# Eight-core decoder trunk: first input and weights without gates, first head in halves, last tile split

## What is computed

```python
def trunk(x, ...):
    for l in range(2):
        h = rmsnorm(x, norm_mix[l])
        if l == 0:   # pool channels (256) and six HGRN heads (128 x 128 state each)
            mixed, p_new, s_new = even_layer(h, ...)   # h @ w_in (1024 x 3328), pooling, recurrence, @ w_out
        else:
            mixed, c_new = odd_layer(h, ...)           # (B * conv3(C * hv)) @ w_out, with h @ w_in (1024 x 3072)
        x = x + mixed
        h = rmsnorm(x, norm_mlp[l])
        x = x + jnp.square(jax.nn.relu(h @ ff_w1[l])) @ ff_w2[l]      # 1024 -> 4096 -> 1024
    return rmsnorm(x, norm_final), ...
```

## Time and profile before

| what | value |
|---|---|
| median of 3 runs | 1538.13 us (1537.94 to 1538.3) |
| the profiled execution | 1537.33 us |
| its span, slowest core (core 4) | 1535.8 us |
| spans of the cores | 1529.1 to 1535.8 us |
| TensorE (PE) busy | 1455.6 us, 95%, 9034 matmuls |
| VectorE (DVE) busy | 887.7 us, 58% |
| ScalarE (ACT) busy | 632.0 us, 41%, 71 table loads of 1.283 us among it |
| GpSimd (POOL) busy | 186.0 us, 12% |
| chain that ended last | PE 90%, ACT 4%, DVE 3%, DMA 1% |

### The profile page before, as it was taken

The page is one execution under the profiler, slowest core; times in us unless marked ns, Lnnn a source line. Parts: engine busy times, 40 slices in busy tenths (PEclk is TensorE's granted clock), DMA queues, the critical chain, the costliest instruction groups (busy, mean ns, idle before and its releaser), DMA issues.

```text
span 1535.8 us, 24078 instructions; the slowest of 8 cores (1529.1 to 1535.8 us)
## 1 busy us (share of the span) xinstructions
PE 1455.6 (95%) x9034; PEld 817.6 (53%) x9034; DVE 887.7 (58%) x1860; ACT 632.0 (41%) x1187; POOL 186.0 (12%) x272
## 2 busy tenths in 40 slices
PE   2789799999999999999999999999999999999996
PEld 1445344554555444444444446666666666666663
DVE  4766686676657768565333368533357767433355
ACT  3788747655797433222212234222133224211132
POOL 1233313001111141100100010001001110001000
PEclk9899799999999999999999999999999999999998
DMA  6835333157346646962633558055245544155222
GB/s 142 183 56 83 56 56 85 28 114 166 83 85 140 152 70 99 174 117 52 110 56 61 104 111 167 15 97 85 51 72 83 95 89 83 25 86 95 52 58 75
DMA packets 49553, 138.56 MB, mean 90 GB/s; under 512 B 7840, under 2 KB 15904, under 8 KB 47904
## 3 DMA queue, kind: packets, MB, share of 16 engines
q0 software_dynamic: 29408, 101.76, 39.9%
q1 hardware_dynamic: 19600, 34.93, 6.9%
q10 hardware_dynamic: 432, 0.33, 0.1%
HBM read 223.21 MB, written 15.54 MB: 155 GB/s over the span
## 4 chain that ended last, share of the span: by engine, by line
PE 90%; ACT 4%; DVE 3%; DMA 1%; issue 1%; POOL 0%; DVEq 0%; SPq 0%; ACTq 0%; POOLq 0%
PE pp L549 89%; ACT arena L494 3%; DVE hT L529 1%; ACT L494 1%; DVE arena L514 1%; DMA x_sb<-xp 1%; DMA ring<-wst 1%; DVE arena L529 0%; POOL arena L514 0%; PE pp L558 0%; DVE arena L542 0%; DVE x_sb L514 0%; ACT mixT L494 0%; DVE mixT L514 0%; DVE mixT L529 0%
## 5 line engine op out<-in xcount | busy, mean ns | idle before, releaser
L549 PE MATMUL pp<-hT,ring 128*128 128x512 bf16 (+3 forms) x4320 | 785.5, 339 | 5.4 <-DVE hT L529 4.5
L549 PEld LDWEIGHTS pp<-hT,ring 128*128 128x128 bf16 x4320 | 408.5, 98 | 346.6 <-issue 24.9
L549 PE MATMUL pp<-mixT,ring 128*128 128x512 bf16 (+2 forms) x3200 | 576.0, 339 | 7.5 <-DVE mixT L514 4.5
L549 PEld LDWEIGHTS pp<-mixT,ring 128*128 128x128 bf16 x3200 | 311.4, 98 | 249.8 <-issue 17.1
L494 ACT ACTIVATE mixT<-pp 128x512 bf16<-128x512 f32 (+2 forms) x320 | 164.6, 514 | 485.2 <-PE pp L549 484.3
L514 DVE TENSOR_TENSOR x_sb<-x_sb,pp 128x512 f32<-128x512 f32 (+3 forms) x384 | 220.7, 579 | 199.0 <-PE pp L549 198.6
L514 DVE TENSOR_TENSOR mixT<-mixT 128x512 bf16<-128x512 bf16 (+2 forms) x320 | 119.3, 376 | 234.8 <-ACT mixT L494 233.9
L564 POOL DMA_DIRECT2D ring<-wst x202 | 107.7, 542 | 971.0 <-PE pp L549 957.2
L494 ACT ACTIVATE arena<-pp 128x512 f32<-128x512 f32 (+9 forms) x261 | 129.2, 508 | 160.2 <-PE pp L549 142.7
L494 ACT ACTIVATE arena<-x_sb 128x512 f32<-128x512 f32 (+3 forms) x184 | 97.6, 538 | 156.7 <-DVE x_sb L514 144.3
L514 DVE TENSOR_TENSOR arena<-arena 128x512 f32<-128x512 f32 (+6 forms) x195 | 114.3, 586 | 23.6 <-ACT arena L494 19.6
(11 more groups left out here) (65 smaller groups left out, 426.1 us busy)
## 6 DMA issues: line engine op xcount, KB each, us to landing
ring<-wst POOLq DMA_DIRECT2D x186, 512.0 KB, 9.0
arena<-st_hgrn SPq DMA_DIRECT2D x6, 1024.0 KB, 5.3
nhs<-arena SPq DMA_DIRECT2D x6, 1024.0 KB, 7.4
x_sb<-xp SPq DMA_DIRECT2D x8, 512.0 KB, 10.7
mixT<-xp SPq DMA_DIRECT2D x8, 512.0 KB, 7.8
ring<-wst POOLq DMA_DIRECT2D x16, 256.0 KB, 7.9
yp<-arena SPq DMA_DIRECT2D x16, 256.0 KB, 10.2
yp<-arena SPq DMA_DIRECT2D x16, 176.0 KB, 1.9
```

Source lines behind the costliest of these rows:

```text
L549: ins = e.matmul(o, l, r, start=s, stop=t)
```

## The change

It has four parts.

- **First input and first weights.** The first 512 tokens get a tensor of their own, xp0, in which what one load fetches is contiguous for each partition. The head weights are laid out by projection, f, i, g, q, 1024 columns each; head 0's come in four loads with a semaphore each. All gates at the start go; the staging of half 1's input (gate_x1) instead waits for head 5's weights, and the small wblk loads go behind head 0's.
- **First norm and first head.** The norm of each half of tile 0 (g_normx) sums its squares in parts by several matmuls; three of its eight products are made on GpSimd. Head 0's projections of tile 0 are made per half. Tile 1's norm adds on GpSimd.
- **Last tile.** In the last step (1728, 2064) becomes (1728, 1952) and (1952, 2064) with TCUT = 1952; both use g_norm_tail, which stores two chunks at a time, the last tile's on SP and ACT in turn, and ys in one store.
- **Planner.** New priorities, DMA rates of 300e3, and HB1 of 4 in place of 6.

The rest are details that keep buffers apart (a few added waits) and the new column offsets. The diff, cut:

```diff
-    PRI = {'norma': 0, 'frontA': 4.6, 'add': 8.7, 'pools': 10.8, 'normy': 59.0, 'cchain': 18.7, 'normc': 0, 'normz': 4.2, 'poolA': 3.1}
+    PRI = {'norma': 15.2, 'frontA': 4.6, 'add': 0, 'pools': 10.8, 'normy': 50.3, 'cchain': 18.7, 'normc': 0, 'normz': 1.3, 'poolA': 3.1, 'relu': 0, 'dense': 21.4, 'normp': 0, 'normd': 4.6, 'poolB': 0, 'normx': 4.5}
-    DMA_RATE = {"sp": 200e3, "act": 200e3, "pool": 270e3}
+    DMA_RATE = {"sp": 300e3, "act": 200e3, "pool": 300e3}
...
+    xp0 = din("xp0", [128, 2, 8, 256])
...
-        ring_ds = [new_dsem(f"ds_ring{i}") for i in range(NSLOT)]
+        ring_ds = [[new_dsem(f"ds_ring{i}_{q}") for q in range(4)] for i in range(NSLOT)]
...
-        HB1 = 6
+        HB1 = 4
...
+                st = 1024 if key == ("H", 0, 0) else 2048
+                for c0 in range(0, unit_cols[u], st):
+                    c1 = min(c0 + st, unit_cols[u])
                     pairs.append((ring[:, s, c0:c1], wst[u, :, c0:c1]))
-                yield DMA("pool", ring_ds[s], pairs, after_, [B_ring[s]], nbytes=unit_cols[u] * 512)
+                if key[0] == "H":
+                    for i, pr in enumerate(pairs):
+                        k = st // 1024
+                        if key == ("H", 0, 5):
+                            gate_x1.extend(B_ring[s])
+                        yield DMA("pool", ring_ds[s][i * k], [pr], after_, B_ring[s][i * k:(i + 1) * k], nbytes=st * 512)
+                else:
+                    yield DMA("pool", ring_ds[s][0], pairs, after_, B_ring[s], nbytes=unit_cols[u] * 512)
...
+            yield WAIT(("ld", ("H", 0, 0)))
             yield DMA("pool", new_dsem("ds_wblk"), [
...
+            if final and b >= (TCUT if TCUT else NTOK):
+                yield from g_norm_tail(n, a, b, xap, xbf, seng)
+                return
...
+        def g_norm_tail(n, a, b, xap, xbf, seng):
+            N = b - a
+            e = min(b, NT) - a
+            NXG = 3
+            pO, pA, pR, *pX = yield GRAB(-(-8 * N // PGW), 1, 1, *[1] * (2 + NXG))
+            pS, pX = pX[:2], pX[2:]
+            acc, BA_ = pgf(pA, N), pgb(pA)
+            yo = pgf(pO, 8 * N).rearrange("p (c t) -> p c t", c=8)
+            BO = [Buf(f"yo{c}") for c in range(8)]
+            yield MEMSET(yo[:, 0, 0:1], 0.0, pgb(pO, -(-8 * N // PGW)) + BO)
+            for c in range(8):
+                yield WAIT(("x", n, a, c))
+                s_, Bs_ = (acc, BA_) if c == 0 else (pgf(pS[c % 2], N), pgb(pS[c % 2]))
+                yield ACT(s_, xap(c), AF.Square, xbf(c), Bs_)
+                if 0 < c < 6:
+                    yield TT(acc, acc, s_, ALU.add, BA_ + Bs_, BA_, eng=seng)
+                if 0 < c <= NXG:
+                    yield ACT(pgf(pX[c - 1], N), xap(c), AF.Copy, xbf(c) + [B_const], pgb(pX[c - 1]), scale=gfin[:, c:c + 1])
+                if c == 5:
+                    (pk,) = yield TAKE(PS)
+                if c >= 5:
+                    yield MMG([(bank(pk)[:, 0:N], onesf, acc if c == 5 else s_, c == 5, c == 7)], (BA_ if c == 5 else Bs_) + [B_const], [B_ps[pk]], passes=4)
+            lt, Bl, rs, Br = pgf(pS[0], N), pgb(pS[0]), pgf(pR, N), pgb(pR)
+            yield ACT(lt, bank(pk)[:, 0:N], AF.Ln, [B_ps[pk]], Bl, scale=1.0 / 1024, bias=EPS)
+            PS.put(pk)
+            yield ACT(rs, lt, AF.Exp, Bl, Br, scale=-0.5)
+            for i in range(4):
+                for c, eng in ((1 + i, "pool"), ((0, 4, 5, 6)[i], "dve")):
+                    if eng == "pool" and i < NXG:
+                        yield TT(yo[:, c, :], pgf(pX[i], N), rs, ALU.mult, pgb(pX[i]) + Br, [BO[c]], eng="pool")
+                    elif eng == "dve":
+                        yield STT(yo[:, c, :], xap(c), gfin[:, c:c + 1], rs, ALU.mult, ALU.mult, xbf(c) + Br + [B_const], [BO[c]])
+            yield STT(yo[:, 7, :], xap(7), gfin[:, 7:8], rs, ALU.mult, ALU.mult, xbf(7) + Br + [B_const], [BO[7]])
+            for i, cs in enumerate(((0, 1), (4, 5), (2, 3), (6, 7))):
+                yield DMA(("sp", "act")[i % 2 if b > NT else 0], y_ds[y_ptr[0] % len(y_ds)],
+                          [(yp[:, cs[0]:cs[1] + 1, a:a + e], yo[:, cs[0]:cs[1] + 1, 0:e])], [BO[c] for c in cs], (), nbytes=e * 1024)
+                y_ptr[0] += 1
+            if b > NT:
+                yield DMA("sp", misc(), [(ys, yo[:, :, e:N])], BO, (), nbytes=65536)
...
             for t, (a, b) in enumerate(HT[0]):
                 m = (a + b) // 2
-                parts = [(a, m), (m, b)] if t == 0 else [(a, b)]
-                for (u, v) in parts:
+                for i, (u, v) in enumerate([(a, m), (m, b)] if t == 0 else [(a, b)]):
                     nq = 2 if t == 0 else 4
                     for q in range(nq):
-                        extra = [B_ring[loaded[("H", 0, 1)]]] if t == 1 and q == 0 else []
                         cs = slice(8 // nq * q, 8 // nq * (q + 1))
-                        yield DMA("sp", x_ds[x_ptr[0]], [(x_sb[:, cs, u:v], xp[:, cs, u:v])], extra,
+                        src = xp0[:, i, cs, :] if t == 0 else xp[:, cs, u:v]
+                        yield DMA("sp", x_ds[x_ptr[0]], [(x_sb[:, cs, u:v], src)], (),
                                   [x for c in range(cs.start, cs.stop) for x in bx(c, u, v)], nbytes=4096 // nq * (v - u))
                         x_ptr[0] += 1
                         for c in range(cs.start, cs.stop):
                             EV.add(("x", 0, u, c))
-                        EV.add(("xl", u, q))
-                    S.spawn(g_norm(0, u, v, *xloc(0, u, v)), 5, f"normx{u}")
-                if t == 0:
-                    yield WAIT(("ld", ("H", 0, 1)))
+                    if t == 0:
+                        S.spawn(g_normx(u, v), 0, f"normp{u}")
+                    else:
+                        S.spawn(g_norm(0, u, v, *xloc(0, u, v), seng="pool"), 5, f"normx{u}")
+
+        def g_normx(a, b):
+            N = b - a
+            xap, xbf = xloc(0, a, b)
+            pA, pS, pT, pU, pV = yield GRAB(1, 1, 1, 1, 1)
+            acc = [(pgf(pA, N, 256 * i), [B_pg[pA][i]]) for i in range(2)]
+            sq = [(pgf(p, N, 256 * i), [B_pg[p][i]]) for p in (pS, pT) for i in range(2)]
+            (pk,) = yield TAKE(PS)
+            if a == 0:
...
+            else:
+                for c in range(8):
+                    s_, Bs_ = sq[c % 4]
+                    yield ACT(s_, xap(c), AF.Square, xbf(c), Bs_)
+                    yield MMG([(bank(pk)[:, 0:N], onesf, s_, c == 0, c == 7)], Bs_ + [B_const], [B_ps[pk]], passes=4)
+            xg = [(pgf(p, N, 256 * i), [B_pg[p][i]]) for p in (pU, pV) for i in range(2)]
+            nx = 3
+            for c in range(nx):
+                yield ACT(xg[c][0], xap(7 - c), AF.Copy, xbf(7 - c) + [B_const], xg[c][1], scale=gcols[:, 7 - c:8 - c])
+            (lt, Bl), (rs, Br) = sq[0], sq[1]
+            yield ACT(lt, bank(pk)[:, 0:N], AF.Ln, [B_ps[pk]], Bl, scale=1.0 / 1024, bias=EPS)
+            PS.put(pk)
+            yield ACT(rs, lt, AF.Exp, Bl, Br, scale=-0.5)
+            for c in range(8 - nx):
+                yield STT(hT[:, c, a:b], xap(c), gcols[:, c:c + 1], rs, ALU.mult, ALU.mult, xbf(c) + Br + [B_const], bh(c, a, b))
+                if c == 0:
+                    EV.add(("hT", 0, a, "s"))
+                if c < nx:
+                    yield TT(hT[:, 7 - c, a:b], xg[c][0], rs, ALU.mult, xg[c][1] + Br, bh(7 - c, a, b), eng="pool")
+            EV.add(("hT", 0, a))
...
-                    yield DMA("sp", stg_ds[q], [(ap[:, 2 * q:2 * q + 2, :], xp[:, 2 * q:2 * q + 2, a:b])], (),
+                    yield DMA("sp", stg_ds[q], [(ap[:, 2 * q:2 * q + 2, :], xp[:, 2 * q:2 * q + 2, a:b])], gate_x1,
...
+            first = (h, t) == (0, 0)
+            if first:
+                Tm = mids[1]
+                kf, ki, kg = yield from htake(half, 3)
+                Bx2 = {k: [Buf(f"fh{k}_{i}") for i in range(2)] for k in (kf, ki, kg)}
+                yield WAIT(("hT", 0, T0, "s"))
+                for kc in range(8):
+                    yield MMG([(bank(kf)[:, 0:Tm - T0], Wr(0, kc), hT[:, kc, T0:Tm], kc == 0, kc == 7)],
+                              [B_ring[sl][0]] + bh(kc, T0, Tm), [B_ps[kf], Bx2[kf][0]])
+                yield proji(ki, T0, Tm, [B_ps[ki], Bx2[ki][0]])
+                yield proj(kg, 2, T0, Tm, [B_ps[kg], Bx2[kg][0]])
+                yield WAIT(("hT", 0, Tm))
+                yield proj(kf, 0, Tm, T1, [B_ps[kf], Bx2[kf][1]])
+            else:
+                (kf,) = yield from htake(half)
+                yield proj(kf, 0, T0, T1, [B_ps[kf]])
...
-            yield WAIT(("front", h, t))
+            yield WAIT(("front", h, t), "const")
...
-                for (a, b) in DT[half]:
+                tiles = [(a, a, b) for (a, b) in DT[half]]
+                if last and n_after == 4 and half == 1:
+                    ta, tb = DT[1][-1]
+                    tiles[-1:] = [(ta, ta, TCUT), (ta, TCUT, tb)]
+                for (ta, a, b) in tiles:
...
```

(36 more changed lines are left out.)

54 lines of the change are left out of this document (40 added, 14 removed).

## The result

The changed kernel takes 1572.9 us (median of 4 runs, 1571.9 to 1578.0) beside 1538.2 (4 runs, 1537.9 to 1539.2) of the kernel before: the ratio is 1.023, 95% interval 1.0217 to 1.0243. It is slower by 35 us where 1531, 7 us faster, was forecast; the range ended at 1545. Some executions, of either kernel, have one die at a lower granted clock and take longer; every time and ratio in this document leaves them out.

A forecast was written before the change was run, and what follows sets the result against it. TensorE was taken as the bound, with the head stage a chain of ScalarE and VectorE steps. Terms: late heads +8, fill -10, body 0, tail -5, sum -7 on the 1538.13 us median, giving 1531; range 1517 to 1545.

The forecast's parts named there:

- Start: From program start to ScalarE's first sigmoid: tile 1's input, slowed by queued weight loads, moves it from 33.5 to 47 us.
- all of it at about 16; head 0's 2 MB take 7 us: Start: tile 0 landed at about 16 us, then head 0's weights; tile 1 follows from 21, in at 43 to 50.
- +13.5: Start: forecast delay in us of ScalarE's first sigmoid, at 47 instead of 33.5.
- The second rival: Start: input isn't held up, tile 1 lands at 29 us, first sigmoid at 31; -23, 1515 us; chance 0.2.
- Given back at once: Start: eight squares of tile 1, 4.9 us on ScalarE, now run in the wait instead of after the first sigmoid.
- Head stage: First sigmoid to heads' end: ends at 196 instead of 188 (+8), output projections filling gaps -10; in sum -2 us.
- The -10: Head stage: output-projection matmuls between last chain steps, 14 us of work in half-idle TensorE time, 4 lost to delayed steps.
- The first rival: Start and head stage: the stall passes through, heads end at 204 (+16); 1543 us, or 1546; chance 0.25.
- +8 for +13.5: Head stage: first sigmoid 13.5 us late, heads' end only 8 us late, with ScalarE at its old 82% share.
- Body: From 190 us on: new priorities and fewer banks reorder nearly everything; taken as 0, bounded by about 4 us either way.
- the marks that I had set for wrong: First sigmoid before 35 us, the chain keeping its full 13 us delay, or TensorE gaps beyond 190 us above 12 us.
- Tail: End of program: 7 instead of 14.8 us after TensorE, 7.8 gained, 2.3 paid in TensorE work; -5 us taken.

The follow-up runs named there:

- e2: The changed kernel with tile 1's norm planned after head 0's first projections, loads unchanged: 1567.5 us, ratio 1.0166 to the kernel before.
- e1: The changed kernel with nine weight loads (heads 1 to 4, pool unit) held until tile 1's input is in: 1558.8 us, ratio 1.0107 to the kernel before.
- e5: As e1, with the adds of tile 1's norm back on VectorE instead of POOL: 1555.2 us, ratio 1.0101 to the kernel before.
- e19: The kernel before, each engine's order kept, the gates on its starting loads taken away: 1550.8 us, ratio 1.0076.
- e13: The changed kernel combining e2 and e5, held loads behind both halves' products: two executions, 1558.2 and 1555.9 us.
- e12: The changed kernel with the old start (gated loads, no halves in first projections, tile 1 normed as before): 1565.1 us, ratio 1.0163 to the kernel before.
- e8: As e3, with the nine weight loads held and tile 1's adds on VectorE: 1560.4 us, ratio 1.0183 to the kernel before.
- e3: The changed kernel with the priorities, DMA rates and HB1 of before: 1562.7 us, ratio 1.0138 to the kernel before.
- e4: The kernel before with only the new tail (TCUT and g_norm_tail): 1539.1 us, ratio 0.9987.

## Why the prediction was wrong

**Start: right mechanism, half the size.** The step "all of it at about 16; head 0's 2 MB take 7 us ... I take 21, then 22 to 29 us more" took tile 0 as landed before the weights count, and let tile 1 alone share. In fact all 3072 input records share with weights. Tile 0's last load landed at 31.8 us, and tile 1's first record went at 25.3 instead of 21 (+4). Its 1024 records took until 58.0, so 33 us instead of the 25.5 that I put in the middle (+7). From there a square and a table load of 1.28 us stood ahead of the sigmoid at 60.38 (+2). Together these are the missing 13.4 us: +27 for ScalarE, not +13.5. The share was read rightly from the earlier trace rows, 1.5 to 1, was too kind.

The Trainium skill's rule on whole packets ("DMA: Bandwidth & Descriptors", "Queues, rings and completion order"), with several input records a turn, is contradicted again for this form, by 867 records to 867 from 24 to 48 us. The second rival's row was misread: of the 720 records in the earlier trace rows, 614 have 64 bytes (the sample tokens, xs), and the large ones go 92 to 72. It says nothing on contiguous sources, and tile 0, whose source is contiguous, was starved as well.

**"Given back at once", 4.9 us, did not come.** The squares run in the wait, as foreseen, but they make the first sigmoid wait for the last load: with them behind head 0's first projections (e2) it comes 15 us earlier. From the first sigmoid to the heads' end ScalarE was still busy for 132.6 us (core 0), where 122.3 were forecast. And I gave POOL's adds no price: e1 and e5 show 5 us of them on ScalarE's path (44.0 against 38.7).

**Head stage: failed.** Eight groups of output projections do stand between the last chain steps, as the order said (208 to 226 us on core 0, 1.89 us each). But TensorE's idle time in 60 to 230 us is 32 us instead of 22, and the heads end at 223 instead of 185, 163 us after the first sigmoid instead of 153. The -10 took TensorE's work for the limit of a stretch whose limit is the chain; how much of the 10 us longer is the chain waiting behind these groups, no run separates. The first rival's passage through the stage is what happened: in e19 the heads' end comes 13.3 us later and the whole 12.1, for +13.5. My forecast that the stage would catch up (+8 for +13.5) had no row behind it but ScalarE's old share, and ScalarE did not get fuller: busy for 132.6 of 163.6 us, 81%, where it was 82%.

**Body: failed.** "I take 0, since the cover, TensorE's dense work, is always there", with 4 us as bound. The idle beyond 230 us rose from 8.6 to 19.7. The bound came from the idle of the old order; a new order brings waits that no row of the old one shows: some 9 us for weights on the slower cores and 3.2 for hT, not for banks. The runs that test the numbers alone (1.0077 to 1.0289, with the first sigmoid unmoved) show that this mistake was as large as that of the start. Of the marks that I had set for wrong, two are there: the delay passes whole, and TensorE's gaps beyond 190 us sum to more than 12.

**Tail: nearly right.** 9.3 us after TensorE instead of 7, +1.5 us of TensorE instead of +2.3: -4 for -5, by the trace of the changed kernel. By itself it is worth -2.9 only once POOL is out of it; POOL's DRAIN was missing from the working.

How they add: the start's 27 us, at nine tenths, are 24, and an order like those of e13 and e12 costs 18 and 25 with the tail's gain in it, together 42 or more; 35 is measured, since ScalarE's wait and the order's gaps partly fall together (e8 against e3 shows it: 19 us of start, nothing at the end). How much of the 35 belongs to which, beyond that, stays open, and the sum is an estimate: the order can't be held fixed under this change, since the code planned is another. So does why the cores part (e1: 1555, 1544, 1557, 1543 ...): 7 to 9 us of waits for weights at 230 to 700 us stand on cores 0 and 2 of e1, 0.4 or less on 1 and 3. Which cores it is changes from run to run.

## What to carry to other kernels

Loads that are asked for early are not free because nobody waits for them: here two queues shared the DMA engines record by record (867 to 867), and the one with the small records starved. Let bulk weights wait for the first input, and count all records of the input, not those of its last piece. Where a planner sets the order, measure first what a meaningless nudge does (here 1%, from one nudge): a smaller gain is easily lost in replanning, and an edit is judged only with the order held, as in e19. And GpSimd's closing DRAIN can outlast work that is moved there in the last microseconds (8.55 us in e4).
